# The delta rule's two lanes of heads, half a head apart instead of in step

## The reference, cut to what matters

```
decay = exp(G_i - G_j) on the lower triangle
lmat  = strict(kb @ k.T * decay)
t_inv = inverse of (lmat + I)               # unit lower triangular
u, w  = t_inv @ (v * beta), t_inv @ (kb * exp(G))
a_qk  = incl(q @ k.T * decay)
# scan over the chunks
v_new = u - w @ state
state = state * chunk_decay + k_dec.T @ v_new
o     = q_dec @ state_before + a_qk @ v_new
```

## Time and profile before

| | us |
|---|---|
| median of 3 runs | 4268.09 (4260.17 to 4273.49) |
| profiled execution, its own time | 4260.88 |
| its span, first to last instruction | 4259.6 |
| granted TensorE clock, mean over the span | 0.941 |
| TensorE busy | 3909.2 (92%) |
| VectorE busy | 2502.5 (59%) |
| ScalarE busy | 1554.9 (37%) |
| GpSimd busy | 867.3 (20%) |

### The profile page before, as it was taken

The page is one execution under the profiler, slowest core; times in us unless marked ns, Lnnn a source line. Parts: engine busy times, 40 slices in busy tenths (PEclk is TensorE's granted clock), DMA queues, the critical chain, the costliest instruction groups (busy, mean ns, idle before and its releaser), DMA issues.

```text
span 4259.6 us, 58496 instructions
## 1 busy us (share of the span) xinstructions
PE 3909.2 (92%) x23644; PEld 3440.6 (81%) x23644; DVE 2502.5 (59%) x5025; ACT 1554.9 (37%) x2353; POOL 867.3 (20%) x404
## 2 busy tenths in 40 slices
PE   7997888899999998999999988899998999776799
PEld 4667777778888887788888876789998999755699
DVE  4554544479507883067766665592943777543475
ACT  2323333333235553221111134444663333432353
POOL 0003333034543333300000000287662000000000
PEclk8998888899999999999999998899999999875799
DMA  5330000123444556467776621257777877321255
GB/s 176 99 122 22 1 1 1 30 84 128 149 147 163 195 196 244 158 201 240 239 245 231 243 85 35 85 181 218 247 243 239 278 266 263 125 71 46 84 159 158
DMA packets 225595, 649.37 MB, mean 152 GB/s; under 512 B 20144, under 2 KB 89648, under 8 KB 217520
## 3 DMA queue, kind: packets, MB, share of 16 engines
q1 hardware_dynamic: 120448, 406.11, 30.3%
q10 hardware_dynamic: 104880, 239.53, 15.6%
HBM read 543.33 MB, written 101.71 MB: 151 GB/s over the span
## 4 chain that ended last, share of the span: by engine, by line
PE 85%; DVE 8%; ACT 4%; POOL 1%; ACTq 1%; DMA 1%; issue 1%; DVEq 0%; POOLq 0%
PE ps L130 84%; DVE g_b L77 2%; PE ps L133 2%; POOL lo L77 1%; ACTq L72 1%; ACT s_s L122 1%; ACT g_b L121 1%; DVE s_s L83 1%; DVE s_st L95 0%; DVE g_b L89 0%; DVE n_rs L98 0%; DVE lo L77 0%; ACT L121 0%; DMA pcA<-pcga 0%; DVE hn_r L98 0%
## 5 line engine op out<-in xcount | busy, mean ns | idle before, releaser
L125 ACT ACTIVATE hi<-ring 128x1024 fp32r<-128x1024 f32 x725 | 767.3, 1059 | 1040.5 <-PE ps L130 930.7
L77 POOL TENSOR_TENSOR lo<-ring,hi 128x1024 fp32r<-128x1024 f32 x288 | 723.2, 2514 | 1770.9 <-ACT hi L125 1770.8
L77 DVE TENSOR_TENSOR lo<-ring,hi 128x1024 fp32r<-128x1024 f32 x437 | 533.1, 1222 | 443.8 <-ACT hi L125 442.9
L130 PE MATMUL ps<-pahh,hi 128*128 128x512 f32 x1152 | 455.4, 395 | 18.8 <-POOL lo L77 11.8
L130 PE MATMUL ps<-pahl,hi 128*128 128x512 f32 x1152 | 450.2, 391 | 0.0
L130 PE MATMUL ps<-pahh,lo 128*128 128x512 f32 x1152 | 449.9, 391 | 0.0
L130 PE MATMUL ps<-pchh,hi 128*128 128x256 f32 x1152 | 337.0, 292 | 25.9 <-POOL lo L77 20.0
L130 PE MATMUL ps<-pchh,lo 128*128 128x256 f32 x1152 | 328.9, 286 | 0.0
L130 PE MATMUL ps<-pchl,hi 128*128 128x256 f32 x1152 | 328.9, 285 | 0.0
L130 PEld LDWEIGHTS ps<-pahh,hi 128*128 128x128 f32 x1152 | 217.6, 189 | 63.7 <-POOL lo L77 12.8
L77 POOL TENSOR_TENSOR g_b<-g_b,g_c 128x512 f32<-128x512 f32 x112 | 143.9, 1304 | 601.8 <-DVE g_b L89 496.4
(11 more groups left out here) (433 smaller groups left out, 9173.0 us busy)
## 6 DMA issues: line engine op xcount, KB each, us to landing
ring<-in_u SPq DMA_DIRECT2D x256, 512.0 KB, 3.7
ring<-in_v SPq DMA_DIRECT2D x256, 512.0 KB, 3.7
paA<-paga ACTq DMA_DIRECT2D x128, 256.0 KB, 2.4
paG<-paR ACTq DMA_DIRECT2D x16, 2048.0 KB, 8.6
paAg<-paA ACTq DMA_DIRECT2D x16, 2048.0 KB, 8.4
paGg<-paG ACTq DMA_DIRECT2D x16, 2048.0 KB, 16.6
late_w<-in_adat ACTq DMA_DIRECT2D x56, 512.0 KB, 3.9
ring<-in_ffn_up SPq DMA_DIRECT2D x44, 512.0 KB, 3.8
```

Of the source, the lines that this page charges most:

```text
L77: return Op(self.e.tensor_tensor(out, a, b, op) if self.real else None)
L125: return Op(self.e.activation(out, a, ACT.Copy, scale=scale) if self.real else None)
L130: return Op(self.e.matmul(out, l, r, start=start, stop=stop, skip_group_check=skip) if self.real else None)
```

## The change

The four calls of `weave` are replaced. Each lane becomes one generator that goes through its heads 0, 2, 4, 6 or 1, 3, 5, 7 without a gap, padded to 32 steps a head. Lane 1 first yields 16 times with no work. What each step of a head does, the buffers and the waits stay as they are; the order in which an engine gets the steps of the two lanes changes.

```
-            weave([tensor(hd) for hd in range(8)], 2)
-            weave([scalar(hd) for hd in range(8)], 2)
-            weave([vector(hd) for hd in range(8)], 2)
-            weave([masks(hd) for hd in range(8)], 2)
+
+            STEPS = 32
+
+            def lane(engine, k):
+                for _ in range(k * STEPS // 2):
+                    yield True
+                for hd in range(k, 8, 2):
+                    n = 0
+                    for _ in engine(hd):
+                        n += 1
+                        yield True
+                    for _ in range(STEPS - n):
+                        yield True
+
+            for engine in (tensor, scalar, vector, masks):
+                weave([lane(engine, k) for k in range(2)], 2)
             meet("gdn_heads")
```

## The result

The changed kernel takes 4313.27 us (median of 4 executions, 4310.62 to 4318.07) against 4264.41 for the kernel before (4 executions). The ratio is 1.0115, 95% interval 1.0103 to 1.0127: slower by about 49 us. I had forecast 4311.5 us, between 4276 and 4330, and a rise of 43.4 us.

What follows compares the result with a forecast made beforehand. TensorE was taken to bound the stage: 323.8 us of records plus waits in beginnings. With 28.8 us for start, end and output and 123.7 for fronts, 476.3 against 432.9: +43.4 on 4268.09 gives 4311.5 us, range 4276 to 4330.

Steps and rivals of the forecast that it cites:

- Inverse beside scan: Passes with one lane in the inverse, the other in the scan: TensorE stays dense as before, gain 0.
- A: Beginnings of heads 1, 3, 5, 7 beside lane 0's inverse: 14.4 us lost each, 18.4 with the clock's fall.
- B: Beginnings of heads 2, 4, 6 beside lane 1's inverse: 12.8 us lost each, 16.7 with the clock's fall.
- My two terms, 18.4 and 16.7: Loss in us per overlapped beginning, A and B, clock fall included; four and three of them, 123.7 us.
- The clock: In overlapped beginnings the clock falls in the long hole, costing 3.9 to 4.0 us each; bounds 0 and 8.
- second hole: TensorE's wait before the other lane's XT: 5.3 us in A, 4.7 in B, after a first of 3.3.
- One lane alone: Head 0's beginning and levels, head 7's end, last output copy, without the other lane: 28.8 us, bounds 20 to 40.
- The port: VectorE's two-SBUF-operand instructions beside GpSimd masks: 0.7 us for each qd, nothing for `kbg` and `kd`; upper bound 30 us.
- rival 3: Masks beside `kbg`, `kd`, qd, X0 and two clock falls a front: up to +73 us, 4341; chance 0.15.
- The clock did not stay up: Rival that the clock stays up in overlapped beginnings, bursts breaking the holes: +15.7 us, 4284; chance 0.22.
- The much slower case: Same as rival 3: port waits in most passes and two clock falls, up to 4341 us; chance 0.15.
- The faster case: Rival that the other lane fills the beginnings: stage 353 us, kernel 4188, under 11.5 us lost each; chance 0.08.

Runs made afterwards that it cites:

- act_later: Changed kernel with a head's exponentials one step later in ScalarE's queue, so the other lane's copies come ahead of them; 4309.98 us, stage 478.5 against 480.3.
- fill_holes: Changed kernel with 11 useless matmuls ahead of Y and 22 ahead of XT in every beginning but the first; 4305.05 us, ratio 1.0079.
- stretch: Changed kernel with beginnings over 17 steps instead of 5, lanes 22 of 44 apart, direction 1's D and DT ahead of direction 0's LM, aq, qd; 4251.90 us.
- stretch9: Changed kernel with beginnings over 9 steps instead of 5, lanes 18 of 36 apart, exponentials in four pieces, direction 1's D and DT early; 4243.15 us, ratio 0.9939.
- spread_first: Changed kernel with VectorE's D and DT of direction 1 ahead of LM, aq and qd of direction 0; 4277.75 us, ratio 1.0025.

## Why the prediction was right

The mechanism held: one serial beginning for each head, eight in place of four. That 4311.5 and 4313.27 lie within 2 us of each other is in part luck. I added 43.4 us to a median of 4268.09, and the kernel before came to 4264.41 beside the changed one: the rise was 48.9 us by the medians and 46.3 by the stage.

**What bounds the stage.** 323.8 us of matmul records, the rest waits in the beginnings. This held: the changed stage is longer by 46 us with the same records, and in it TensorE waits for over 0.9 us at a time only in beginnings and in head 7's end.

**Inverse beside scan: gain 0.** It held. In the changed kernel head 1's first exponentials start at 402.51, head 3's at 519.38, 116.9 us later, and two heads' records are 81.0 us. So one A and one B beginning together lose 35.9 us, and for the later pairs 35.3 and 34.9 (starts at 635.66 and 751.52). My two terms, 18.4 and 16.7, give 35.1; at most 0.8 is left over for the dense part. Directly: between 478.0 and 518.5 us TensorE is busy for 39.9 of 40.5 us.

**The beginnings.** For A I had Y6, XT6 and w at 12.2, 19.3 and 27.7 us, the last 29.4 with the 0.8 and 0.9 of the slow clock; they came at 12.3, 19.5 and 29.6. The windows above give 29.5 and 27.3 us for the two patterns. The sentence that explained it, though, was half right. "The other lane cannot use the time, since its next step waits in the same queues" is true of the holes as they are, but act_later frees both waits and gains nothing clear. The chain of one head with five steps beside it is the cause; the queues decide only where the hole shows.

**The clock.** I took it to fall in the second hole. In head 1's beginning it fell in the first already (0.77 at 404 us; Y6 took 3.75 us). In head 2's it fell in the second only:
```profile
461.16 2.02 PE L130 MATMUL ps<-g_b,g_b 128*128 128x128 f32 x16 [3.14 <-ACT g_b L125]
467.58 3.78 PE L130 MATMUL ps<-g_b,g_b 128*128 128x128 f32 x16 [4.40 <-ACT g_b L125]
```

This is no matter of the pattern: the Y behind the first hole takes 2.02 us in five of the seven beginnings, 3.75 in head 1's and 2.48 in head 5's, while the XT behind the second hole takes 3.78 us in all seven, as I had it. The slow Y6 is hidden, since its copies wait for ScalarE anyway. So the term was right in its place and, by the rows of head 1's beginning, near in size: 4.5 us estimated against my 3.9 to 4.0. As a saving, fill_holes shows only 1.5 us of it.

**One lane alone.** The term was mis-sized. A level of head 0 alone takes 5.2 us (copies at 377.40 and 382.60), not 4.94. Head 7's end was 4.5 us lost in my sum. TensorE's timeline there:
```profile
809.73 2.01 PE L130 MATMUL ps<-g_b,g_b 128*128 128x128 f32 x16
813.24 3.50 PE L130 MATMUL ps<-g_b,g_b 128*128 128x128 f32 x18 [1.51 <-DVE g_b L77]
822.81 0.49 PE L130 MATMUL ps<-n_xn,g_b 128*128 128x128 f32 x2
825.49 0.49 PE L130 MATMUL ps<-g_b,n_xn 128*128 128x128 f32 x2
```

The chunks of the scan are 2.68 us apart (822.81 to 825.49), not 2.39, and the 18 records of w take 3.50 us, at half clock. From head 6's last o, at about 797.6, to the last matmul at 826.5 there are 28.9 us, and head 7 still has 196 records then, 21.8 us: 7.1 lost, not 4.5. With 0.25 us more for each of four levels that is 3.6 us too little in my sum. Head 0's beginning went the other way: 23.8 us (348.1 to 371.9) for the 24.5 in the sum. What remains is 2.9 us, as much as the stage's 46.3 exceed my 43.4; that it fits to a tenth is chance.

**The port.** I counted 0.7 us for each qd over the 0.68 it takes alone, and they took 1.39 and 1.38 in head 1's beginning of the changed kernel, as before. The Trainium skill (SBUF — State Buffer, Who interferes with whom) has the two instructions exclude one another. The trace agrees, and the price it shows is 0.70 us, about the part of the mask still to run (qd begins at 407.11, the mask ends at 407.95), not the whole 1.26. The long ones of rival 3 did not come: all 32 of `kbg` and `kd` took 0.68 to 0.69 us, 0.6 apart (2.49 us for four at 422.61). But the price I set on them is real: in `stretch`, where the lanes meet otherwise, `kbg` and `kd` of three heads took 1.8 and 1.1 us more a pair.

**The rivals.** The clock did not stay up. The much slower case is out. The faster case asked for less than 11.5 us lost in a beginning; the changed kernel loses 17 to 18. stretch9 has 409.2 - 323.8 = 85.4 us besides its records; with my 28.8 us for start, end and output that leaves 8.1 us for each of seven, on the other side of that point, and it is faster.

## What to carry to other kernels

Two lanes in step pay a serial beginning once for both; set apart, they pay it for each, and it can be hidden only if the other lane has as much work in the steps that stand beside it as the chain is long. That is not enough by itself, as `stretch` shows. So before a lag is set, lay the chain of the thin part beside the matmul time of the steps that the written order puts next to it: here 25 us beside 12 to 13. If it does not fit, lengthen the beginning in steps (stretch9) or shorten its chain (spread_first), and look then for the engine whose work has been pushed together.

## What was not expected of the hardware

The granted clock fell in a hole that had begun at 402.9 us and was down within the window 404 to 406, about 2 us later, where in the kernel before it took 3 to 4; a hole of the same length in the next beginning left it at full, and in head 5's it fell only 4.5 us after TensorE had stopped, in the Y behind the hole. Matmuls that fill such holes kept it at 1.00 (414 to 416 us in fill_holes), and it fell again between 418 and 420, about 4 us after XT6 had ended, with one flip in between.
